# Modulation rows repeated over partitions by TensorE, layer 1's modulation weights streamed during the projections, and layer 0's first two expert visits fixed

## What is computed

```python
def _modulate(x, gain, shift, scale):
    return _rms_norm(x, gain) * (1 + scale[:, None, :]) + shift[:, None, :]

def _adaln(c, w, b, n):
    return jnp.split(jax.nn.silu(c) @ w + b, n, axis=-1)

for layer in range(DEPTH):
    sh1, sc1, g1, sh2, sc2, g2 = _adaln(c, ada_w[layer], ada_b[layer], 6)
    # layer 0: pooling mixer; layer 1: shared keys and values from a norm of its own
    # (_adaln(c, kv_ada_w, kv_ada_b, 2)), then attention
    h = _modulate(x, norm_g[layer, 0], sh1, sc1)
    x = x + g1[:, None, :] * mixer(h)
    h = _modulate(x, norm_g[layer, 1], sh2, sc2)
    x = x + g2[:, None, :] * _moe(h, ...)
```

## Time and profile before

| what | us |
|---|---|
| median of 3 runs (lowest, highest) | 1436.46 (1422.54, 1446.48) |
| the profiled execution: its time | 1439.3 |
| the profiled execution: span from first to last instruction | 1437.7 |
| TensorE busy in the span | 1159.8 (81%) |
| VectorE busy | 463.1 (32%) |
| ScalarE busy | 240.3 (17%) |
| data moved | 359.00 MB, mean 250 GB/s |

### The profile page before, as it was taken

The page is one execution under the profiler, slowest core; times in us unless marked ns, Lnnn a source line. Parts: engine busy times, 40 slices in busy tenths (PEclk is TensorE's granted clock), DMA queues, the critical chain, the costliest instruction groups (busy, mean ns, idle before and its releaser), DMA issues.

```text
span 1437.7 us, 15209 instructions
## 1 busy us (share of the span) xinstructions
PE 1159.8 (81%) x5484; PEld 633.6 (44%) x5484; DVE 463.1 (32%) x1085; ACT 240.3 (17%) x541; POOL 137.5 (10%) x234
## 2 busy tenths in 40 slices
PE   2528857999989974999995888778962999999990
PEld 0016532444434432444554777655432444444440
DVE  3043662011100117264136667322357001111105
ACT  2002100111100114211122444221120001111101
POOL 4100001001010002000002000111000000110002
PEclk9768778999999996999997999878985999999995
DMA  9996769999999963312515000645141799999955
GB/s 362 404 394 253 299 249 343 409 413 414 409 397 410 413 240 123 111 59 62 184 59 158 6 0 0 199 114 201 59 183 34 270 365 385 413 406 407 403 186 194
DMA packets 69301, 359.00 MB, mean 250 GB/s; under 512 B 9693, under 2 KB 11181, under 8 KB 54346
## 3 DMA queue, kind: packets, MB, share of 16 engines
q1 hardware_dynamic: 44800, 285.79, 50.4%
q0 software_dynamic: 17920, 66.33, 13.8%
q10 hardware_dynamic: 6538, 6.31, 1.3%
HBM read 333.78 MB, written 28.56 MB: 252 GB/s over the span
## 4 chain that ended last, share of the span: by engine, by line
PE 71%; DVE 14%; DMA 7%; issue 3%; ACTq 2%; ACT 2%; POOL 1%; DVEq 0%; POOLq 0%; SPq 0%
PE pb L812 17%; PE pb L998 16%; PE pb L854 9%; PE pb L816 7%; PE pb L862 3%; PE pb L1092 2%; PE pb L806 2%; PE pb L745 2%; DMA gainb<-in_norm_g_dram 2%; DMA adab<-in_ada_b_dram 1%; DMA h<-h_d,idx 1%; DMA ada_d<-stage 1%; PE pb L1137 1%; DVE ring L2005 1%; PE pb L1069 1%
## 5 line engine op out<-in xcount | busy, mean ns | idle before, releaser
L812 PE MATMUL pb<-ring,h 128*128 128x512 f32 x576 | 259.5, 600 | 3.5 <-DVE h L1790 2.5
L998 PE MATMUL pb<-ring,hT_raw 128*128 128x512 f32 x512 | 225.4, 598 | 1.3 <-DVE hT_raw L1566 0.8
L812 PEld LDWEIGHTS pb<-ring,h 128*128 128x128 f32 x576 | 106.9, 192 | 125.2 <-issue 124.0
L998 PEld LDWEIGHTS pb<-ring,hT_raw 128*128 128x128 f32 x512 | 97.0, 192 | 116.7 <-issue 115.6
L1804 DVE COPY hT_raw<-pb 128x512 f32<-128x512 f32 (+1 forms) x32 | 22.1, 692 | 339.4 <-PE pb L854 203.2
L854 PE MATMUL pb<-ring,hT_raw 128*128 128x512 f32 x288 | 128.0, 597 | 0.0
L731 PE MATMUL pb<-ring,cT 128*32 128x512 f32 x448 | 67.0, 739 | 58.8 <-DMA ring<-in_ada_w_dram 25.0
L816 PE MATMUL pb<-ring,h 128*64 128x256 f32 x896 | 106.0, 384 | 0.0
L854 PEld LDWEIGHTS pb<-ring,hT_raw 128*128 128x128 f32 x288 | 53.6, 190 | 67.6 <-issue 67.6
L816 PEld LDWEIGHTS pb<-ring,h 128*64 128x64 f32 x896 | 60.6, 137 | 42.2 <-issue 14.5
L1799 DVE TENSOR_TENSOR h<-pb,h 128x512 f32<-128x512 f32 (+1 forms) x32 | 18.4, 575 | 157.5 <-PE pb L812 115.9
(11 more groups left out here) (322 smaller groups left out, 1309.5 us busy)
## 6 DMA issues: line engine op xcount, KB each, us to landing
ring<-in_w_gate_dram SPq DMA_DIRECT2D x32, 2048.0 KB, 11.9
ring<-in_w_up_dram SPq DMA_DIRECT2D x32, 2048.0 KB, 12.6
ring<-in_w_down_dram SPq DMA_DIRECT2D x32, 2048.0 KB, 13.7
ring<-in_ada_w_dram SPq DMA_DIRECT2D x24, 2048.0 KB, 10.4
ys_d<-hT_raw POOLq DMA_DIRECT2D x18, 512.0 KB, 8.0
ring<-in_kv_ada_w_dram SPq DMA_DIRECT2D x4, 2048.0 KB, 13.2
ring<-in_w_kvf_dram SPq DMA_DIRECT2D x4, 2048.0 KB, 8.9
mod<-ada_d POOLq DMA_DIRECT2D x14, 512.0 KB, 6.5
```

The costliest lines, as they stand in the source:

```text
L812: return T.matmul(bank[:, :], xgT[:, par, k, :], w[:, k * DE:(k + 1) * DE], start=(k == 0), stop=(k == KC - 1))
L998: last = T.matmul(bank[:, :], hT[:, k, col[t]:col[t] + P], w[:, k * 512:(k + 1) * 512], start=(k == 0), stop=(k == KC - 1))
```

## The change

1. **Repeating by TensorE.** For groups 0 to 2 nothing goes to DRAM. `stage_ada` adds the bias and multiplies the gain in (or the pool scale, into the gate) while the rows still lie in `stage`; `spread` multiplies `stage[32j:32j+32]` by a matrix that has ones in the row of the prompt, so that a bank holds the row in all 128 partitions; `spread_sample` does the same for the sample's 32. ScalarE and VectorE copy the banks into `mod`. The gains are loaded small (eight rows) beside the bias. For groups 3 to 6 the way through DRAM stays, with the gain multiplied in before the store; `scale_ready` is gone.
2. **Fewer units ahead of the experts.** Only units 0 to 15 (groups 0 to 3) go through the ring. x is loaded ahead of unit 0. Group 2 is made during the tile loop, group 3 during `route` and behind it.
3. **Units 16 to 27 later.** They go into two spare areas of 2 MB, loaded by SyncE between blocks 1 and 2 of the projections, from `yg_loaded[2]` on, and are multiplied on TensorE between the products 0 to 9. Units 16 to 19 share one area; from 20 on they alternate.
4. **Second-stage norms behind the loop.** VectorE's five norms of stage 1 now follow the whole tile loop.
5. **First visits fixed.** Experts 0 and 1 come first in layer 0 too; their five weight blocks are loaded as the ring's slots come free.
6. **Queues.** The small loads (router, biases, head gains) move from ScalarE's queue to GpSimd's, behind its constants; ScalarE computes silu(c) first.

```diff
+    NEARLY = 16
+    ada_slot = [n % 6 for n in range(NEARLY)]
+    spare_of = [0 if n < NEARLY + 4 or n % 2 else 1 for n in range(NADA)]
...
-            load(0, ada_src[0])
-            load(1, ada_src[1])
             for t in range(TP):
                 sp.dma_start(x[:, t, :], x_prompt[0, t * P:(t + 1) * P, :]).then_inc(x_loaded, 16)
...
-            for n in range(2, NADA):
+            for n in range(NEARLY):
...
-                if layer == 0:
-                    sp.wait_ge(perm_ready, 1)
-                    e01 = [expert_of(0), expert_of(1)]
-                    order = ["g0", "u0", "g1", "d0", "u1"]
...
+                e01 = [0, 1]
+                order = (["d0", "g0", "g1", "u0", "u1"], ["u0", "d0", "u1", "g0", "g1"])[layer]
...
+                if n == 2:
+                    sp.wait_ge(E.down, 2 * NE)
+                    sp.wait_ge(yg_loaded[2], 32)
+                    for u in range(NEARLY, NADA):
+                        b = spare_of[u]
+                        earlier = [m for m in range(NEARLY, u) if spare_of[m] == b]
+                        if earlier:
+                            sp.wait_ge(unit_used, earlier[-1] + 1)
+                        elif b == 1:
+                            sp.wait_ge(combined, NT)
+                        sp.dma_start(spare[b].rearrange("p (k n) -> p k n", k=2), ada_src[u]).then_inc(spare_loaded[b], 16)
...
-            link(g.memset(kbias[:, 1, 0:1], 1.0e6))
-            link(g.memset(kbias[:, 1, 1:2], 2.0e6))
+                link(g.memset(kbias[:, layer, 0:1], 1.0e6))
+                link(g.memset(kbias[:, layer, 1:2], 2.0e6))
...
+            def spread(bank, grp, j):
+
+                return T.matmul(bank[:, :], selp[32 * j:32 * j + 32, :], stage[32 * j:32 * j + 32, grp % 2, :],
+                                start=True, stop=True, tile_position=(32 * j, 0))
...
-            for grp in range(3):
-                ada(grp)
...
+            ada(0)
+            pe.wait_ge(bands_ready, 1)
+            pe.wait_ge(ada_staged, 1)
+            for j in range(4):
+                last = spread(pb[2 + j], 0, j)
+            last.then_inc(bc_done, 1)
+            spread_sample(pb[6], 0)
+            ada(1, [0, 1])
...
             differences(0)
+            ada(1, [2, 3])
+            pe.wait_ge(ada_staged, 2)
+            for j in range(2):
+                spread(pb[6 + j], 1, j).then_inc(bc_done, 1)
...
-                if t < 4:
-                    ada(3, [t])
-            ada(4, [0, 1])
+                if t != 2:
+                    ada(2, [t - t // 3])
+            pe.wait_ge(ada_staged, 3)
...
             route(0)
-            ada(4, [2, 3])
-            ada(5, [0, 1])
+            ada(3, [2, 3])
             ranks(0)
-            ada(5, [2, 3])
             slots_to_tokens(0)
-            ada(6)
-            pe.wait_ge(ada_staged, 7)
+            pe.wait_ge(ada_staged, 4)
             experts(0)
...
+            ada(4, [0, 1])
             h_transposed(1, 2, 0)
             for t in range(NT):
                 if t + 1 < NT:
                     h_transposed(1, 2, t + 1)
                 project(t)
+                if t < 2:
+                    ada(4, [2 + t])
+                elif t < 4:
+                    ada(5, [t - 2])
+            pe.wait_ge(ada_staged, 5)
+            narrow_product(2, (0, 7), 1, partT_f, f_done)
             for c in range(NT, 2 * NT):
                 project(c)
+                if c < NT + 2:
+                    ada(5, [c - NT + 2])
+                    if c == NT + 1:
+                        ada(6, [0])
+                elif c < 2 * NT:
+                    ada(6, [c - NT - 1])
...
+                V.scalar_tensor_tensor(out=stage[part, grp % 2, :], in0=stage[part, grp % 2, :],
+                                       scalar=1.0 if plus_one else 0.0, in1=gainr[part, grp % 2, :],
+                                       op0=ALU.add, op1=ALU.mult).then_inc(ada_staged, 1)
...
-                if t == 2:
-                    scale_ready(1)
-                if t >= 2:
-                    norm_tile(1, 2, t - 2)
...
-            stage_ada(3)
-            for t in range(TP - 1, NT):
+            stage_ada(2)
+            modulation_ready(1)
+            for t in range(NT):
                 norm_tile(1, 2, t)
...
             pick(0)
+            stage_ada(3)
             places(0)
-            stage_ada(4)
-            stage_ada(5)
-            stage_ada(6)
             experts(0)
```

More of the change, by code:

```diff
@@ L247, in bass_yoco_stream_step @@
         ada_staged = sem("ada_staged")
-        ada_stored = [sem(f"ada{i}_stored") for i in range(7)]
+        ada_stored = [None] * 3 + [sem(f"ada{i}_stored") for i in range(3, 7)]
         ab_loaded = sem("ab_loaded")
-        a_ready = sem("a_ready")
+        gain_loaded = [sem(f"gain{i}_loaded") for i in range(2)]
+        stage_sum = sem("stage_sum")
+        bc_done = sem("bc_done")
+        bc_act = sem("bc_act")
+        bc_dve = sem("bc_dve")
+        bands_built = sem("bands_built")
+        pool_loaded = sem("pool_loaded")
+        spare_loaded = [sem(f"spare{i}_loaded") for i in range(2)]
         g_loaded = sem("g_loaded")
-        gp_ready = sem("gp_ready")
-        adab_zero = sem("adab_zero")
+        zeroed = sem("zeroed")
         qk_sq = sem("qk_sq")
@@ L427, in first @@
                     if layer == 0:
-                        last = max(n for n in range(NADA) if ada_slot[n] == slot)
+                        last = max(n for n in range(NEARLY) if ada_slot[n] == slot)
                         sp.wait_ge(unit_used, last + 1)
@@ L445, in turn @@
                     load_weights(U_SLOT + par, wu_v, e, slot_loaded[U_SLOT + par])
[L447 to L456 removed]
+                e01 = [0, 1]
+                order = (["d0", "g0", "g1", "u0", "u1"], ["u0", "d0", "u1", "g0", "g1"])[layer]
+                for kind, v in order:
                     first(kind, int(v), e01[int(v)])
@@ L780, in route @@
                     h_transposed(6 * layer, 4 * layer or 1, t)
+                    if layer == 0 and t % 2 == 0 and t < TS:
+                        ada(3, [t // 2])
                 s = 6 * layer * NT
@@ L1181, in load_bias @@
                                 src[0][src[1]:src[1] + 2048].rearrange("(j n) -> j n", j=4)).then_inc(bias_loaded[grp % 2], 16)
+                if GAINS[grp] is not None:
+                    j0, gain, _ = GAINS[grp]
+                    for s in range(2):
+                        A.dma_start(gainr[32 * j0 + s:32 * j0 + 64:32, grp % 2, :],
+                                    gain.rearrange("(j n) -> j n", j=2)).then_inc(gain_loaded[grp % 2], 16)
             def store_ada(grp):
@@ L1834, in experts @@
                         V.tensor_copy(ysb[:, 0, 512:1024], pb[6][:, :]).then_inc(ov_dve[layer], 1)
-                dve.wait_ge(g_loaded, (80, 144)[layer])
                 if layer == 0:
-                    scale_ready(2)
+                    dve.wait_ge(bc_act, 20)
+                    modulation_ready(2)
+                else:
+                    dve.wait_ge(g_loaded, 64)
                 for t in range(NT):
```

242 lines of the change are left out of this document (162 added, 80 removed).

## The result

| | us |
|---|---|
| after: median of 20 runs (lowest, highest) | 1442.06 (1436.73, 1449.83) |
| before: median of 20 runs of the same series (lowest, highest) | 1434.05 (1420.54, 1449.55) |
| ratio, 95% interval | 1.0077 [1.0053, 1.0101] |
| after, profiled execution: time, span | 1438.74, 1436.7 |

The changed kernel is 8 us slower: under 2%, but the interval excludes no change. The time lies in the predicted range (1411 to 1450), 10 us above the predicted 1432. The median of 20 puts before at 1434.05, another 2.4 us lower.

The account below looks back on a forecast made before the run. Bound: small transfers beside full DMA up to the first norm, then TensorE, VectorE's routing and a busy TensorE from 236 us. Span 1437.7 - 41 + 36 = 1432.7, execution 1434.3, less 2.8: 1432 us; range 1411 to 1450 (8 in 10).

Parts of the forecast that it names:

- The visits: Layer 0's sixteen expert visits: same sizes, so length left at 298 us; a gather's wait might give 0 to 7.5.
- the spread of the three runs: Three runs of the kernel before differ by 24 us; one reason given for the range 1418 to 1446.
- Up to the first up product: Start of the kernel to the first expert product: first norm at 45 us, first expert product at 195, 41 earlier.
- 0 to 7.5 of gain, and I take 0: In the visits: possible gain from the one gather waiting 7.5 us behind the filling of result rows; counted as 0.
- Behind the experts: From the last expert product through projection products 0 to 9: product 0 16 us late, product 10 36 late.
- Block 2: Projection weights queued past unit 27: issued at about 654, landing 667, when product 10 is due; costs 1 us.
- The sum: Whole kernel: span 1437.7 - 41 + 36 = 1432.7, execution 1434.3, less the profile's distance from the median: 1432.
- the correction to the median: In the sum: profiled execution of before lies 2.8 us above the median of the runs, so 1434.3 becomes 1431.5.
- Units that hide: Rival, projections: units fall into waits or tile 0's wait shrinks, 23 of 36 us go: 1409; chance 0.12.
- Load-bound projections: Rival, behind the experts: single area and 13.2 us loads delay tile 0 and ten units: 1457; chance 0.08.
- extra block: Rival, layer 0's experts: one token too many in a small visit adds about 45 us: 1477; chance 0.03.

Follow-up runs that it names:

- e8: The kernel before, unchanged, profiled once more; 1431.79 us.
- e1: The changed kernel with no unit ahead of tile 0, all twelve late units behind the projection products; 1437.73 us, ratio to before 1.0013.
- e7: The changed kernel with layer 0's first two visits picked by the lists again; 1439.86 us, ratio to before 1.0028.
- e4: The changed kernel with all 28 units ahead of the experts, repetition by TensorE and fixed first visits kept; 1413.80 us, ratio to before 0.9852.
- e10: The kernel before, unchanged, profiled another time; 1422.46 us.
- e11: The changed kernel, unchanged, profiled once more; 1446.27 us.

## Why the prediction went wrong

Two steps failed. The visits were left at their length before (275.4 us) and took 281.9 and 280.9; and the sum was made from one profiled execution of before, shifted by its distance of 2.8 us from the median, although that distance lay in the stretch that the change removes. The first is more than the forecast gain of 4.5 us, the second 2.8 of it. The other terms, by far the larger ones, held. That 1442 still lies in the range is in part luck: the range had nothing for longer visits, and what covers them is the width taken from the spread of the three runs.

**Up to the first up product: right.** First norm 47.15 (45 forecast), group 1 staged at 61.7 (62.2), first pool product 75.1 (77.6), lists 184.4 (186.0), first up product 193.5 and 195.9 (195). The spreads took 2.09 us at a granted clock of 0.50 for all four, against the 3.4 taken. Since the units of group 1 were the later ones, it moved nothing. The Trainium skill ("TensorE: Matmul & The Clock Gate", Measured speedup vs the span model) gives 3.07 for four row tiles, by which the estimate was 2.5 at the low clock; the trace is a little shorter still.

**The visits: wrong.** "I leave them at 298", and "0 to 7.5 of gain, and I take 0". The bound had no upper side: the argument was that the DMA is a little less behind. Measured: 6.5 and 5.5 us longer (281.9 and 280.9 against 275.4). In the first trace 2.8 are the first up product, 9.96 us rather than 7.13, because TensorE had run only 2.87 of the 10 us ahead of it and the granted clock was 0.50; in before, units of group 6 stood there. 3.1 are the gather, 10.6 rather than 7.5. The wait was not a rest of some fixed size but one gather behind a copy in a queue on full engines; e8 shows it at 10.3 in before too. That it was 7.1 to 7.5 in three of before's four profiles and 10.1 to 11.4 in those of after, e1 and e7 is measured; why the changed kernel sits at the upper end is not shown.

**Behind the experts: right.** Gap and products together grew by 37.7 us in the first trace and 37.9 in the second, with 36 forecast: product 0 17.4 us late (16), ten units at 1.9 and 1.3 to 1.5 more (20). The loads were 9.70 and 7.33 rather than twice 8. (The prediction's estimate of 7.2 rests on the Trainium skill ("DMA: Bandwidth & Descriptors", Anatomy of one DMA), which fits its fixed 2 us to transfers issued by GpSimd. These are SyncE's, so 7.33 is near the estimate but no test of the page.) Block 2 was issued right behind the last unit, took 13.68 us to land (13 forecast) and cost 0.9 us (1). e4 confirms the term by taking it away (-37.1), e1 shows that the loads behind it have next to no slack.

**The sum: the correction to the median was wrong.** I took 2.8 off because before's profiled execution lay 2.8 above the median. But the four profiles show that before's executions differ above all in the first norm's start, 14 us, and that is the stretch which the change removes: time less first norm is the same to 8.4 us, in three of the four to 3.2. Of an execution with an early start the change takes away less. The changed kernel has no such two kinds, so nothing was to be taken off its sum, and its gain counts from before's mixture: at the start 42.4 us against the kind with 94.7, but 25.8 against e10 (219.3 less 193.5). On medians of 20 the result is +8. Left uncorrected, the sum gave 1434.3, that is no change against before's 1434.05.

The 10 us between 1432 and 1442.06 are then: 2.3 for this correction (2.8 less 0.5 of rounding), 4.4 between the forecast 1434.3 and the profiled 1438.74 (visits +6.5, gap and products +1.7, start -1.4, rest -2.8, which is 4.0, and 0.4 outside the span), and 3.3 by which that execution lies below its median; e11, with the rest at 681.2, is 4.2 above it. The prediction took the rest as unchanged; it was 2.8 below and 3.2 above before's 678.0, with the granted clock in layer 1's attention (e11).

**The rivals.** Units that hide fell (89.45 of 92 us busy between 546 and 638). Load-bound projections fell in after, with 0.9 us of waits for weights, and came up in part in e1. No extra block ran: it would stand in the gap at some 45 us, and e1's gap, with the same fixed visits, is 53.0 as before.

## What to carry to other kernels

In this kernel work taken off a stretch with idle engines and put on a full one was paid twice, as work and as waits for its loads: first look where TensorE and the queues are both idle (here beside the routing) and put it there. When the change removes the stretch in which executions of the old kernel differ, profile the old one several times and don't shift the forecast by the distance of one profile from its median. Fill or copy jobs that share a queue with gathers belong behind the last gather: here that gave 5.8 us of the span, 12.5 in the visits less 4.7 in what follows them and a start 2.2 later.

## What the runs showed of the hardware

A small store of eight rows beside full DMA engines (share 1.02 from 47 to 94 us in each) took 5.65, 6.29, 8.74, 15.04 or 19.27 us in five executions whose kernels have the same code up to there. A gather of token rows landed in 4.5 us at the least (the shortest of three in before, issued from 215.5 to 235.2 us; the DMA share was 0.54 from 215 to 221) and in 22.69 behind the filling's copies, the larger of 1.8 MB, in the same queue, while the engines moved about 400 GB/s. Four spreads with a contraction over 32 rows each, on four row groups of TensorE, took 2.09 us at the low clock, where four products one after another were put at up to 7.7 (an estimate; no run has them so). In layer 1's attention the granted clock from 20 to 180 us behind product 29 was 0.88 to 0.92 over 14 executions, and the time from product 29 to the end went with it, 681.2 to 674.7 us.
